# Scores by blocks of 32 keys, earlier stores of y, and x's tiles given up in pairs, in a hybrid decoder layer

## The chip, the cores and the metric

The kernel runs on one core of one Trainium2 chip. The metric is the device time of one execution in microseconds. Every fence marked as profile shows lines of a hardware profile of one execution.

## What is computed

One decoder layer (depth 1) for 512 prompt tokens and 8 x 8 sample tokens, 576 tokens (T) together, model width 2048, everything in float32:

```
xn   = RMSNorm(x)
proj = xn @ w_in                        # q, k, v, g, low-rank gate, z, x/B/C, dt
GLA (4 heads, key 128, value 256):
  b   = cumsum(log-gate) inside a chunk
  att[t,s] = sum_k q[t,k] * exp(b[t,k]-b[s,k]) * k[s,k]     for s <= t only
  o   = q*exp(b) @ S + att @ v,  S carried from chunk to chunk
SSD (16 heads of 64, state 128): the same kind of chunked scan, then norm
mix  = [o ; y] @ w_out ;  h = x + RMSNorm(mix)
out  = h + RMSNorm((silu(conv(h_n @ ffn_in))_a * (...)_b) @ ffn_out)
```

The kernel works with chunks of 128 tokens. The change concerns the matrix `att` of each chunk and head, the storing of y (the output of the SSD part) and its loading back for `@ w_out`.

## The kernel before, in words

**Main stream.** TensorE runs one long stream of projection products: for a tile of 128 output channels, 16 k-tiles of x (8 per "unit"), each with three products in fp32r (w_hi x_hi, w_hi x_lo, w_lo x_hi; lines 944 and 946) over two halves of 288 tokens. So a unit is 48 matmuls. Weights come by DMA from SyncE (line 361), ScalarE makes `w_hi` (line 441), GpSimd makes `w_lo` (line 383), in a ring of four slots. `units_done` counts finished units.

**Gaps.** The 32 tiles z, q, k, g, v (loop over `n < BESIDE`) have 63 "gaps", one after each unit, in which the small work of SSD and GLA is put into TensorE's stream. Every engine has its own `gap(m)` function with its part of gap m; `before_gap` puts small pieces between the k-tiles. Order on each engine is program order. ScalarE's queue also issues DMAs. An issue of a DMA waits in program order, but does not wait until the activations ahead of it have run.

**Scores.** In gaps 37, 39, ..., 51 `att_step(s)` (line 1109), s from 0 to 7, makes for each of 4 heads and 4 chunks one plain float32 matmul of 128 keys by 128 queries (line 1121). Step 0 is the diagonal. Step s multiplies operands scaled to a reference at block size m = LEVELS[s-1] = 64, 32, 16, 8, 4, 2, 1: only queries in the upper half of a block of 2m with keys in the lower half are wanted. VectorE takes those by a predicated copy with mask s (`take_att`, line 1670) and leaves the rest of PSUM unread. A float32 matmul of the program appears as two MATMUL records and two LDWEIGHTS records.  Four of the steps have a small part for the sample tokens too (line 1128).

**y.** `y_high(g)` (ScalarE, line 567) makes the high parts of four tiles of y; low parts come from GpSimd (line 402) for g = 0 and VectorE (line 1814) for g = 1. In gap 32 ScalarE does `y_high(0)`, `gates()` (the gate logits out of PSUM, lines 560 and 561, TensorE's part at line 1104), `y_high(1)`. In gap 33 come exp and ln of the gate. In gap 34 `y_low_out(0)`, `y_low_out(1)` store the low parts (line 571, 1152 KB each). In gap 35 `load_over_y(0)`, `load_over_y(1)` load q and k from `spill` over the place of the low parts (line 584; each waits until its own low part has landed in `y_spill`), and then `y_high_out(0)`, `y_high_out(1)` store the high parts (line 575). `att_step(0)` waits for q and k (`qk_in`, 32).

**y back.** The output projection reads y from the first eight k-tiles of `x_hi`/`x_lo`. SyncE waits at line 368 until the last unit that reads x's tiles 0 to 7 is done (`units_done`, OUT_UNIT0 - 1; it is the first half of tile n = 31), and then issues eight loads of 576 KB, in four pairs of k-tiles (lines 371 and 373), ahead of the next weights. TensorE's first `half_tile` of the output projection waits for pair k/2 before k = 0, 2, 4, 6. Between these two stands the second unit of tile 31, which reads x's tiles 8 to 15.

Of the kernel before, what the change touches and what calls it, by code (L numbers as in the profile page):

```python
# [52 lines left out]
CH = 128  # L53
# [56 lines left out]
def build(nc, xT, weights, vecs, ident_d, masks_d, gate2, sconv_in, fconv_in, fvec_d, gla_in,  # L110
# [4 lines left out]
    with ExitStack() as ctx:  # L115
# [151 lines left out]
        sq_ready, sq_used = sem("sq_ready"), sem("sq_used")  # L267
        root_ready = sem("root_ready")
        rstd_ready = sem("rstd_ready")
        gate_mm, gate_out, gate_exp, gate_ln = (sem(n) for n in ("gate_mm", "gate_out", "gate_exp", "gate_ln"))  # L270
        b_ready = sem("b_ready")
        v_tr, v_out = sem("v_tr"), sem("v_out")
        spilled = [sem("spilled0"), sem("spilled1")]
# [72 lines left out]
        @block.sync  # L346
        def _(sp):

            sp.dma_start(xin[0], xT[0]).then_inc(x_in[0], 16)
            sp.dma_start(raw[:, 0], weights[0]).then_inc(raw_in[0], 16)  # L350
            sp.dma_start(xin[1], xT[1]).then_inc(x_in[1], 16)
            sp.dma_start(raw[:, 1], weights[1]).then_inc(raw_in[1], 16)
            for c in (2, 3):
                sp.dma_start(xin[c], xT[c]).then_inc(x_in[2], 16)

            def weights_in(start, stop):

                with sp.Fori(start, stop) as i:
                    for j in range(2):
                        sp.wait_ge(lo_ready, 2 * i + j - 1)  # L360
                        sp.dma_start(raw[:, j], weights[bass.ds(2 * i + j, 1)].rearrange("o p a b -> (o p) a b"))\
                            .then_inc(raw_in[j], 16)

            weights_in(1, (OUT_UNIT0 + 4) // 2)
            sp.wait_ge(y_kept, 32)
            for g in range(SG):
                sp.wait_ge(ylo_kept[g], 16)
            sp.wait_ge(units_done, OUT_UNIT0 - 1)
            for i in range(4):
                a, z = 2 * i, 2 * i + 2  # L370
                sp.dma_start(x_hi[:, a:z, :].bitcast(F32), y_spill[0, a:z].rearrange("n p t -> p n t"))\
                    .then_inc(yb_in[i], 16)
                sp.dma_start(x_lo[:, a:z, :].bitcast(F32), y_spill[1, a:z].rearrange("n p t -> p n t"))\
                    .then_inc(yb_in[i], 16)
            weights_in((OUT_UNIT0 + 4) // 2, UNITS // 2)
# [59 lines left out]
        def _(act):  # L435
# [136 lines left out]
                    .then_inc(ylo_kept[g], 16)  # L572

            def y_high_out(g):
                act.dma_start(y_spill[0, 4 * g:4 * g + 4].rearrange("n p t -> p n t"), yh[:, 4 * g:4 * g + 4, :])\
                    .then_inc(y_kept, 16)

# [38 lines left out]
            def gap(m):  # L616
# [37 lines left out]
                if m == GAP_GATE:  # L654
                    for j in range(2):
                        act.wait_ge(hs_out[j], 16 * BATCHES // 2)
                    y_high(0)
                    gates()
                    y_high(1)
                if m == GAP_GATE + 1:  # L660
                    act.wait_ge(gate_out, GH)
                    nc.scalar.activation(GE2, GE2, ACT.Exp, scale=-1.0).then_inc(gate_exp, 1)
                    act.wait_ge(gate_exp, 1)
                    nc.scalar.activation(GE2, GE2, ACT.Ln, bias=1.0).then_inc(gate_ln, 1)
                if m == GAP_GATE + 2:
                    for g in range(SG):
                        y_low_out(g)
                if m == GAP_GATE + 3:
                    for g in range(SG):
                        load_over_y(g)  # L670
                    for g in range(SG):
                        y_high_out(g)
                if GAP_ATT <= m < GAP_ATT + 14 and (m - GAP_ATT) % 2 == 0:
                    level((m - GAP_ATT) // 2 + 1)
                if m == GAP_ATT + 14:
# [261 lines left out]
        def _(pe):  # L937
# [9 lines left out]
                                          start=False, stop=last)  # L947
                return mm

            def project(tile, unit, slot, ring, split=HALF, before=None, middle=None, behind=2, between=None):  # L950

                pe.wait_ge(taken, tile - behind + 3)
                for half in range(2):
# [3 lines left out]
                    for k in range(8):  # L957
                        kt = 8 * half + k
                        if before:
                            before(kt)  # L960
                        mm = products(slot + half, k, ring, split, kt == 0, kt == KT - 1, x_hi[:, kt], x_lo[:, kt])
                        if k == 7:
                            mm.then_inc(units_done, 1)
                        if between:
                            between(half, k)

# [129 lines left out]
            def gate(h):  # L1096
# [9 lines left out]
                                          misc[32:32 + RANK, n * HALF:(n + 1) * HALF], start=True, stop=True)  # L1106
                mm.then_inc(gate_mm, 1)

            def att_step(s):

                k, q = (GKK, GQ) if s == 0 else (GE, GE) if s % 2 else (GE2, GE2)
# [6 lines left out]
                for h in range(GH):  # L1118
                    for c in range(NC):
                        at = h * T + c * CH  # L1120
                        mm = nc.tensor.matmul(work[:, h, c * CH:(c + 1) * CH], k[:, at:at + CH], q[:, at:at + CH],  # L1121
                                              start=True, stop=True)
                    mm.then_inc(att_mm, 1)
                if s in SAMPLE_STEPS:
                    pe.wait_ge(att_out, att_base(s) + 1)
# [157 lines left out]
            for n in range(BESIDE):  # L1283
                tile = N_TILE0 + n
                project(tile, 2 * tile, 2 * tile % 4, tile % 2, middle=(lambda: gap(2 * n - 1)) if n else None,
                        between=lambda half, k: before_gap(2 * n - 1 + half, k))
                gap(2 * n)


# [149 lines left out]
        def _(ve):  # L1439
# [205 lines left out]

            def gates():

                ve.wait_ge(gate_ln, 1)
                own(tt_op(GE, GB, GE2, ALU.subtract))
                settle()  # L1650

# [538 lines left out]
```

## Time and profile before

| | us |
|---|---|
| median of 3 runs | 2717.47 (2716.44 to 2717.69) |
| the profiled execution, time | 2718.59 |
| its span | 2716.4 |
| TensorE matmul, busy | 2670.3 (98%) |
| VectorE, ScalarE, GpSimd busy | 45%, 28%, 39% |

Busy times are those of records; matmuls are pipelined, so a record (0.29 us) is longer than the distance to the next start (0.13 us). Below, the distance between starts is what a matmul costs. Idle time is time with no record open on an engine, and the profile names what it takes to have ended it.

### The profile page before, as it was taken

How to read it: one execution, taken by the hardware profiler on the slowest of the kernel's cores; microseconds unless marked ns; L12 is line 12 of the kernel's file. 1: busy time of each engine (PE TensorE's matmuls, PEld its weight loads, DVE VectorE, ACT ScalarE, POOL GpSimd, SP SyncE). 2: the span in 40 equal slices, each digit the busy share in tenths (PEclk: the TensorE clock that was granted, in tenths of full speed). 3: DMA queues.
4: the chain of work that ended last, by engine and by line, in shares of the span. 5: the costliest groups of instructions: out<-in, count | busy, mean ns of one | idle time of the engine just before them, and what ended most of it. 6: DMA issues, size and time to landing. Idle time of an engine off the chain costs nothing.

```text
span 2716.4 us, 48489 instructions
## 1 busy us (share of the span) xinstructions
PE 2670.3 (98%) x20130; PEld 2644.1 (97%) x20130; DVE 1218.1 (45%) x1459; ACT 763.0 (28%) x1225; POOL 1052.4 (39%) x458
## 2 busy tenths in 40 slices
PE   8999999999999999999999999999999999999996
PEld 7999999999999999999999999999999999999996
DVE  6644544654236354444333443444333443444436
ACT  6232222423214234222222222222222222222222
POOL 3332222423223354344433343444433443434347
PEclk9999999999999999999999999999999999999998
DMA  5222246422453423232222222222222222232224
GB/s 177 78 92 88 80 156 212 177 63 72 138 207 95 148 82 126 78 94 85 80 78 86 78 85 87 78 94 86 81 77 84 78 89 83 78 94 86 86 78 167
DMA packets 84645, 277.04 MB, mean 102 GB/s; under 512 B 9072, under 2 KB 13808, under 8 KB 83584
## 3 DMA queue, kind: packets, MB, share of 16 engines
q1 hardware_dynamic: 58336, 211.84, 24.8%
q10 hardware_dynamic: 26144, 62.64, 6.3%
q8 instruction: 148, 2.42, 0.4%
q14 instruction: 17, 0.14, 0.0%
HBM read 242.80 MB, written 31.65 MB: 101 GB/s over the span
## 4 chain that ended last, share of the span: by engine, by line
issue 44%; PE 31%; POOL 19%; DVE 2%; DMA 2%; ACT 1%; POOLq 0%; SPq 0%; ACTq 0%; DVEq 0%
POOL w_lo L383 18%; PE psum_proj L944 17%; PE psum_proj L946 8%; PE psum_work L1121 1%; POOL arena L414 1%; POOL arena L431 1%; DMA x_lo<-y_spill 1%; DVE arena L1875 1%; PE psum_work L1092 1%; POOL arena L422 1%; PE psum_work L1082 0%; DMA arena<-spill 0%; PE psum_work L1192 0%; DMA out_ssd_s_dram<-arena 0%; PE psum_work L1047 0%
## 5 line engine op out<-in xcount | busy, mean ns | idle before, releaser
L383 POOL TENSOR_TENSOR w_lo<-raw,w_hi 128x1024 fp32r<-128x1024 f32 x386 | 978.2, 2545 | 1642.4 <-ACT w_hi L441 1636.4
L944 PE MATMUL psum_proj<-x_hi,w_hi 128*128 128x288 f32 (+2 forms) x3104 | 934.8, 301 | 19.4 <-DVE x_lo L1464 13.0
L944 PE MATMUL psum_proj<-x_lo,w_hi 128*128 128x288 f32 (+2 forms) x3104 | 916.3, 295 | 0.0
L946 PE MATMUL psum_proj<-x_hi,w_lo 128*128 128x288 f32 (+2 forms) x3104 | 915.8, 295 | 0.0
L441 ACT ACTIVATE w_hi<-raw 128x1024 fp32r<-128x1024 f32 x386 | 398.0, 1053 | 892.4 <-PE psum_proj L946 494.9
L944 PEld LDWEIGHTS psum_proj<-x_hi,w_hi 128*128 128x128 f32 x3104 | 588.3, 190 | 27.6 <-issue 15.5
L944 PEld LDWEIGHTS psum_proj<-x_lo,w_hi 128*128 128x128 f32 x3104 | 584.9, 188 | 3.4 <-issue 1.9
L946 PEld LDWEIGHTS psum_proj<-x_hi,w_lo 128*128 128x128 f32 x3104 | 584.5, 188 | 0.0
L944 PE MATMUL psum_work<-x_lo,w_hi 128*128 128x256 f32 (+1 forms) x1408 | 414.7, 294 | 0.0
L944 PE MATMUL psum_work<-x_hi,w_hi 128*128 128x256 f32 (+1 forms) x1408 | 414.5, 294 | 0.0
L946 PE MATMUL psum_work<-x_hi,w_lo 128*128 128x256 f32 (+1 forms) x1408 | 414.4, 294 | 0.0
L840 ACT ACTIVATE arena<-arena 128x592 f32<-128x592 f32 x88 | 77.8, 884 | 747.3 <-DVE arena L1949 747.3
L944 PEld LDWEIGHTS psum_work<-x_hi,w_hi 128*128 128x128 f32 x1408 | 267.0, 190 | 0.0
L946 PEld LDWEIGHTS psum_work<-x_hi,w_lo 128*128 128x128 f32 x1408 | 264.3, 188 | 0.0
L944 PEld LDWEIGHTS psum_work<-x_lo,w_hi 128*128 128x128 f32 x1408 | 264.2, 188 | 0.0
L1947 DVE TENSOR_TENSOR arena<-psum_proj,rstd 128x512 f32<-128x512 f32 x44 | 30.4, 691 | 428.7 <-PE psum_proj L946 428.7
L944 PE MATMUL psum_proj<-g_lo,w_hi 128*128 128x288 f32 x672 | 198.3, 295 | 0.0
L944 PE MATMUL psum_work<-g_lo,w_hi 128*128 128x288 f32 x672 | 198.2, 295 | 0.0
L946 PE MATMUL psum_proj<-g_hi,w_lo 128*128 128x288 f32 x672 | 198.1, 295 | 0.0
L946 PE MATMUL psum_work<-g_hi,w_lo 128*128 128x288 f32 x672 | 198.1, 295 | 0.0
L944 PE MATMUL psum_work<-g_hi,w_hi 128*128 128x288 f32 x672 | 197.3, 294 | 0.1
L944 PE MATMUL psum_proj<-g_hi,w_hi 128*128 128x288 f32 x672 | 197.1, 293 | 0.0
(311 smaller groups left out, 3249.4 us busy)
## 6 DMA issues: line engine op xcount, KB each, us to landing
raw<-in_weights_dram SPq DMA_DIRECT2D x386, 512.0 KB, 3.6
spill<-tail ACTq DMA_DIRECT2D x24, 288.0 KB, 2.1
arena<-in_xT_dram SPq DMA_DIRECT2D x4, 1152.0 KB, 10.6
y_spill<-arena ACTq DMA_DIRECT2D x4, 1152.0 KB, 10.8
h_spill<-arena ACTq DMA_DIRECT2D x4, 1152.0 KB, 4.5
x_hi<-h_spill ACTq DMA_DIRECT2D x1, 4608.0 KB, 17.8
out_yT_dram<-arena ACTq DMA_DIRECT2D x8, 576.0 KB, 3.5
arena<-in_ssdT_in_dram ACTq DMA_DIRECT2D x8, 512.0 KB, 5.9
```

Source lines behind the costliest of these rows:

```text
L383: nc.gpsimd.tensor_tensor(w_lo[:, slot], raw[:, r], w_hi[:, slot].bitcast(F32), ALU.subtract).then_inc(lo_ready, 1)
L414: nc.gpsimd.tensor_tensor(mixT[:, kt], mixT[:, kt], xres(kt), ALU.add).then_inc(h_w, 1)
L422: nc.gpsimd.tensor_tensor(cut(fsum, n), cut(fsq[0] if kt == 1 else fsum, n), cut(fsq[kt % 2], n), ALU.add).then_inc(ysq_sum, 1)
L431: nc.gpsimd.tensor_tensor(a, a, cut(x_hi[:, kt].bitcast(F32), n), ALU.add).then_inc(y_wp, 1)
L441: nc.scalar.activation(w_hi[:, slot], raw[:, r], ACT.Copy).then_inc(hi_ready, 1)
L840: nc.scalar.activation(ftap[j % 2][:, 0:FCONVW], pd[:, 0:FCONVW], ACT.Identity, bias=fc[q][:, 4 * j + 3:4 * j + 4], scale=fc[q][:, 4 * j:4 ...
L944: nc.tensor.matmul(banks[:, n, 0:b - a], w_hi[:, slot, k], (hi, lo)[part][:, a:b], start=first and part == 0, stop=False)
L946: mm = nc.tensor.matmul(banks[:, n, 0:b - a], w_lo[:, slot, k], hi[:, a:b], start=False, stop=last)
L1092: mm = nc.tensor.matmul(work[:, j // 4, j % 4 * SN:(j % 4 + 1) * SN], xw[0:SMP, j * P:(j + 1) * P], Bm[:, b, j // 4, :], start=True, stop= ...
L1121: mm = nc.tensor.matmul(work[:, h, c * CH:(c + 1) * CH], k[:, at:at + CH], q[:, at:at + CH], start=True, stop=True)
L1875: nc.vector.reciprocal(r, r).then_inc(grs, 1)
L1947: tt_op(pd[:, FC - 1:FC - 1 + SEQ].rearrange("p (n t) -> p n t", n=2), banks[:, :, 0:256], rstd[:, 0:SEQ].rearrange("p (n t) -> p n t", n= ...
```

## The change

Three parts, in the diff in this order of lines.

(a) Stores of y. `y_high_out(0)` follows `y_high(0)` at once, `y_low_out(0)` follows the gates, `y_high_out(1)` follows `y_high(1)`, `y_low_out(1)` comes behind exp and ln in gap 33, `load_over_y(0)` is in gap 34, `load_over_y(1)` in gap 35. A wait for `yhi` is put before each store of a high part, and one semaphore is reused for exp and ln.

(b) Scores. `att_step` makes, in place of one matmul of 128 keys by 128 queries, 2 or 4 matmuls of up to 32 keys: for m = 64 two of 32 keys by 64 queries; for m = 32 two of 32 by 32; for smaller m four of (32 - m) by (32 - m); for step 0 four of 32 by 32. All contract over 128 rows.

(c) x's tiles. In the first unit of tile 31 `x_read` is raised behind k = 1, 3 and 5, and SyncE waits for it before pairs 0, 1 and 2; pair 3 waits for `units_done` as before.

```diff
-            sp.wait_ge(units_done, OUT_UNIT0 - 1)
             for i in range(4):
                 a, z = 2 * i, 2 * i + 2
+                sp.wait_ge(*((x_read, i + 1) if i < 3 else (units_done, OUT_UNIT0 - 1)))
                 sp.dma_start(x_hi[:, a:z, :].bitcast(F32), y_spill[0, a:z].rearrange("n p t -> p n t"))\
                     .then_inc(yb_in[i], 16)
...
             def y_high_out(g):
+                act.wait_ge(yhi, 4 * g + 4)
                 act.dma_start(y_spill[0, 4 * g:4 * g + 4].rearrange("n p t -> p n t"), yh[:, 4 * g:4 * g + 4, :])\
                     .then_inc(y_kept, 16)
...
                     y_high(0)
+                    y_high_out(0)
                     gates()
+                    y_low_out(0)
                     y_high(1)
+                    y_high_out(1)
                 if m == GAP_GATE + 1:
                     act.wait_ge(gate_out, GH)
-                    nc.scalar.activation(GE2, GE2, ACT.Exp, scale=-1.0).then_inc(gate_exp, 1)
-                    act.wait_ge(gate_exp, 1)
+                    nc.scalar.activation(GE2, GE2, ACT.Exp, scale=-1.0).then_inc(gate_ln, 1)
+                    act.wait_ge(gate_ln, 1)
                     nc.scalar.activation(GE2, GE2, ACT.Ln, bias=1.0).then_inc(gate_ln, 1)
+                    y_low_out(1)
                 if m == GAP_GATE + 2:
-                    for g in range(SG):
-                        y_low_out(g)
+                    load_over_y(0)
                 if m == GAP_GATE + 3:
-                    for g in range(SG):
-                        load_over_y(g)
-                    for g in range(SG):
-                        y_high_out(g)
+                    load_over_y(1)
...
+                        if given_up and half == 0 and k in (1, 3, 5):
+                            mm.then_inc(x_read, 1)
...
+            def kept_blocks(s):
+
+                m = LEVELS[s - 1] if s else 0
+                if m == 64:
+                    return [(a, a + 32, 64, CH) for a in (0, 32)]
+                if m == 32:
+                    return [(a, a + 32, a + 32, a + 64) for a in (0, 64)]
+                return [(a, a + 32 - m, a + m, a + 32) for a in (0, 32, 64, 96)]
...
                         at = h * T + c * CH
-                        mm = nc.tensor.matmul(work[:, h, c * CH:(c + 1) * CH], k[:, at:at + CH], q[:, at:at + CH],
-                                              start=True, stop=True)
+                        for a, z, a_q, z_q in kept_blocks(s):
+                            mm = nc.tensor.matmul(work[a:z, h, c * CH + a_q:c * CH + z_q], k[:, at + a:at + z],
+                                                  q[:, at + a_q:at + z_q], start=True, stop=True)
                     mm.then_inc(att_mm, 1)
...
-                ve.wait_ge(gate_ln, 1)
+                ve.wait_ge(gate_ln, 2)
```

## Rows read from the trace of the kernel before

**Rows 1.** The page's first part: each engine's busy us, share of the span, instructions.
```profile
PE 2670.3 (98%) x20130; PEld 2644.1 (97%) x20130; DVE 1218.1 (45%) x1459; ACT 763.0 (28%) x1225; POOL 1052.4 (39%) x458
```

**Rows 2.** Whom TensorE waited for, one line: us in total, times, longest us.
```profile
PE psum_proj L944 <- DMA x_lo<-y_spill: 4.4, 2, 3.5
```

**Rows 3.** TensorE's timeline around score step 1: start us, us, engine, line, operation, count.
```profile
542.05 3.73 PE L1121 MATMUL psum_work<-arena 128*128 128x128 f32 x32
545.54 0.38 PE L944 MATMUL psum_proj<-x_hi,w_hi 128*128 128x288 f32 x1
```

**Rows 4.** TensorE's timeline, matmuls with 64 columns of weights on alternating halves of PSUM's rows.
```profile
247.64 1.09 PE L1043 MATMUL psum_work<-arena 128*64 128x128 f32 x16
248.66 1.12 PE L1047 MATMUL psum_work<-tail,arena 128*128 128x512 f32 x2
...
385.32 0.30 PE L944 MATMUL psum_proj<-x_lo,w_hi 128*128 128x288 f32 x1
385.45 0.29 PE L946 MATMUL psum_proj<-x_hi,w_lo 128*128 128x288 f32 x1
385.68 1.15 PE L1069 MATMUL psum_work<-arena 64*64 64x64 f32 x32
386.76 0.40 PE L944 MATMUL psum_proj<-x_hi,w_hi 128*128 128x288 f32 x1
```

**Rows 5.** TensorE's timeline, short transposes (16 rows, 16 columns moving), two of ten.
```profile
200.45 0.21 PE L1234 MATMUL psum_work<-ident,tail 16*128 16x16 f32 x1
200.51 0.21 PE L1234 MATMUL psum_work<-ident,misc 16*128 16x16 f32 x1
```

**Rows 6.** ScalarE's queue and engine, gaps 34 and 35.
```profile
504.56 1.19 ACTq L571 DMA_DIRECT2D y_spill<-arena  x2
...
511.90 4.41 ACTq L584 DMA_DIRECT2D arena<-spill  x2
```

**Rows 7.** Line 571's own view: time from issue to landing of its two stores.
```profile
DMA to landing us min/median/max: 7.3/9.1/10.8
```

**Rows 8.** The issues view: KB each, median us to landing.
```profile
arena<-spill ACTq DMA_DIRECT2D x2, 1152.0 KB, 8.3
```

**Rows 9.** TensorE's timeline, score step 0 with the idle time before it.
```profile
524.36 3.81 PE L1121 MATMUL psum_work<-arena 128*128 128x128 f32 x32 [2.01 <-POOL w_lo L383]
```

**Rows 10.** Two windows: busy of PE, PEld, DVE, ACT, POOL, then granted clock, DMA share, GB/s.
```profile
500.00:504.00 4.00, 4.00 (x33) 4.00 (x32) 2.10 (x4) 3.97 (x3) 3.02 (x1) 1.00 0.00 0
...
508.00:512.00 4.00, 4.00 (x32) 4.00 (x31) 3.96 (x2) 1.53 (x2) 3.46 (x1) 1.00 1.05 413
```

**Rows 11.** Timeline of gap 32: ScalarE's high parts and first gate copies, TensorE's third gate matmul.
```profile
487.86 2.41 ACT L567 ACTIVATE arena<-arena 128x576 fp32r<-128x576 f32 x4 [1.53 <-DVE tail L1856]
...
490.80 0.73 ACT L561 ACTIVATE tail<-psum_work,vec 128x576 f32<-128x576 f32 x1
...
491.80 1.23 PE L1104 MATMUL psum_work<-misc,tail 16*128 16x288 f32 x4
```

**Rows 12.** SyncE's queue: the last weights before y (two issues), and the first load of y.
```profile
721.94 15.93 SPq L361 DMA_DIRECT2D raw<-in_weights_dram  x2
742.45 0.40 SPq L371 DMA_DIRECT2D x_hi<-y_spill  x1
```

**Rows 13.** TensorE's timeline where the output projection begins, rows with idle time.
```profile
756.11 0.40 PE L944 MATMUL psum_proj<-x_hi,w_hi 128*128 128x288 f32 x1 [0.91 <-DMA x_lo<-y_spill]
...
762.20 0.40 PE L944 MATMUL psum_proj<-x_hi,w_hi 128*128 128x288 f32 x1 [3.46 <-DMA x_lo<-y_spill]
```

**Rows 14.** Windows, columns as in rows 10, at the output projection and at the mix norm.
```profile
755.00:762.20 7.20, 2.84 (x22) 2.65 (x21) 0.00 (x0) 0.00 (x0) 0.00 (x0) 1.00 1.04 413
...
762.84:769.76 6.92, 6.92 (x33) 6.92 (x31) 3.75 (x6) 1.06 (x1) 2.38 (x1) 0.51 0.25 67
...
988.00:992.00 4.00, 4.00 (x21) 3.59 (x19) 0.34 (x4) 0.20 (x2) 0.39 (x1) 0.57 0.43 131
```

**Rows 15.** TensorE's timeline before the second of those: one-column matmuls.
```profile
986.03 1.45 PE L1335 MATMUL psum_work<-ones,tail 128*128 128x1 f32 x12 [0.71 <-DVE tail L1902]
```

More of the change, by code:

```diff
@@ L269, in build @@
         rstd_ready = sem("rstd_ready")
-        gate_mm, gate_out, gate_exp, gate_ln = (sem(n) for n in ("gate_mm", "gate_out", "gate_exp", "gate_ln"))
+        gate_mm, gate_out, gate_ln, x_read = (sem(n) for n in ("gate_mm", "gate_out", "gate_ln", "x_read"))
         b_ready = sem("b_ready")
@@ L948, in products, with project @@
                 return mm
-            def project(tile, unit, slot, ring, split=HALF, before=None, middle=None, behind=2, between=None):
+            def project(tile, unit, slot, ring, split=HALF, before=None, middle=None, behind=2, between=None,
+                        given_up=False):
                 pe.wait_ge(taken, tile - behind + 3)
@@ L1285, in _ @@
                 project(tile, 2 * tile, 2 * tile % 4, tile % 2, middle=(lambda: gap(2 * n - 1)) if n else None,
-                        between=lambda half, k: before_gap(2 * n - 1 + half, k))
+                        between=lambda half, k: before_gap(2 * n - 1 + half, k), given_up=n == BESIDE - 1)
                 gap(2 * n)
```

## The prediction

> **What bounds the kernel now.** First the page's shares: TensorE's matmuls are open for 98% of the span, every other engine is under half [rows 1]. So time can come only from TensorE's own instructions, from its few idle stretches, and from its clock. Then the view of whom TensorE waited for, cut to the two waits near the change: 4.4 us for the loads of y [rows 2] and 2.0 us ahead of a score step [rows 9]. Then the timeline and the windows there, for what these waits are made of.
>
> The 2.0 us stand before score step 0 [rows 9]. The profile names GpSimd's `w_lo`, but I read them as a wait for k. ScalarE's two low stores go out at 504.56 and about 505.1, and the second takes 10.8 us to land [rows 6, 7], so 515.9. The two loads of q and k are 4.41 us apart though one issue takes 0.4 us [rows 6]: the second is held until its low part has landed, and goes out near 515.9. With 8.3 us to land [rows 8] it is there at 524.2, and TensorE starts at 524.36 [rows 9]. The DMA engines are full at this time (share 1.05, 413 GB/s) [rows 10].
>
> The 4.4 us are two waits of the first half tile of the output projection, 0.91 and 3.46 us [rows 13]. SyncE issued the first load at 742.45, and the last data are there at 762.2; the end of that stretch is DMA at 413 GB/s [rows 12 to 14]. A cost follows that no list of waits shows: behind the 3.46 us of idleness the granted clock is 0.51 for 6.92 us [rows 14], the lower of the two levels (1.2 GHz for 2.4).
>
> **Part (b), the scores.** Before: a step of 16 float32 matmuls, 32 records, takes 545.54 - 542.05 = 3.49 us, 109 ns each [rows 3]; eight steps are 27.9 us, all in TensorE's stream and so all on the path. After: steps 0 and 3 to 7 have 16 x 4 matmuls, 128 records, steps 1 and 2 have 16 x 2, 64 records; 896 records in place of 256. Less work, many more instructions: with 0.1 us for the entry of each step (below), 896 t + 0.8 us = 27.9 us holds at t = 30 ns. All hangs on t.
>
> No row shows a float32 matmul with 32 columns of weights. The nearest have 64 and alternate between two halves of PSUM's rows: with 64 columns moving 32 records take 386.76 - 385.68 = 1.08 us, 34 ns each; with 128 moving 16 take 248.66 - 247.64 = 1.02 us, 64 ns each [rows 4]. That is 0.47 ns for a moving column and 4 ns fixed, or 19 ns at 32 columns and 12 ns at 16; over the widths here (16 to 32) some 17 ns. So 34 ns is the upper end, 17 ns the lower. The lower one supposes that no price per instruction shows up first; the upper is measured, with twice the columns. I take 25 ns, the middle. For step 1 (64 columns moving) I take the row's 34 ns. Entering a narrow group costs more: 385.68 - 385.45 = 0.23 us where two starts are else 0.13 us apart [rows 4]; so 0.1 us for each step. Leaving shows in both kernels.
>
> At 25 ns: six steps of 128 x 25 ns + 0.1 = 3.30 us, less by 0.19 each, -1.1; step 1 is 64 x 34 ns + 0.1 = 2.28, -1.2; step 2 is 64 x 25 ns + 0.1 = 1.70, -1.8. Sum **-4.1 us**. At 17 ns it is -10.8, at 34 ns for all +3.4. VectorE still takes a head after TensorE's signal for it and is 45% busy, so nothing there becomes late.
>
> The Trainium skill ("TensorE: Matmul & The Clock Gate", the section on why a gap is 56 and not 53.3 ns) says that starts never come closer than about 25 ns, and, where firmware decodes, that the sequencer spends about 62 ns on each matmul. By the first, part (b) would be near the -4.1 us. By the second a step of 128 would be 7.9 us and the kernel would be slower by some 19 us. The 34 ns of rows 4 speak against the second, but only over 32 matmuls, which may have stood decoded ahead; this is the first rival below, priced there from a row.
>
> **Part (a), the stores.** Nothing is added to the DMA traffic; 4.6 MB move earlier. The first high store goes out when the high parts are made, at 487.86 + 2.41 = 490.3, the first low one behind the gates near 496, the second high one near 500, the second low one near 505 as before, since it now stands behind exp. There is free DMA time before: 500 to 504 shows none used at all in the window view, and the engines fill only from 508 on [rows 10]. The low store of part 1 now shares them with the q load alone, and I let it land in 6 us (between 10.8 and the low end of 7.3 less a share of the traffic [rows 7]): 511. The k load goes out then and takes at most the 8.3 us of now [rows 8]: 519.3. TensorE asks for it at 524.36 - 2.01 = 522.35. So the **2.0 us go**, with 3 us to spare; if only 1 us of the 4.9 came, all would stay. What is late next there is nothing that I find: weights (next in ScalarE's queue) arrive sooner in the emptier DMA.
>
> What it costs: ScalarE's sequencer now waits for `yhi` and issues a DMA (about 0.55 us, half of the 1.09 to 1.19 us for two [rows 6]) between the high parts and the gate copies. Queued behind are all of `gates()`. The first head's copies end at 490.80 + 0.73 = 491.53 today, and TensorE's third gate matmul, which waits for them, starts at 491.80 [rows 11]: 0.27 us of slack. Copies 0.75 us later make TensorE wait **0.5 us** (0 to 0.8). The other added issues stand before `w_hi`, which is units ahead of TensorE; they cost nothing while that lead lasts, up to 0.6 us each if not. Part (a): **-1.5 us** (-2.0 to +0.5).
>
> **Part (c), x's tiles.** SyncE's last weight issue before y ends at 721.94 + 15.93 = 737.87 [rows 12], then it waits 4.6 us. Pair 0, 1 and 2 are given up 6, 4 and 2 k-tiles before the end of the unit, each at least 6 x 0.13 = 0.8 us: before 737.4, 739.0 and 740.6. So pairs 0 to 2 go out between 737.9 and 741.6 and only pair 3 at 742.45. Data to move until then: eight loads of 576 KB, 4.7 MB, and 1 to 1.5 MB of weights and states. At 413 GB/s [rows 14] 4.7 + 1.5 = 6.2 MB are 15 us from 737.9, so the last lands by 753, 9 us before now. TensorE needs pair 0 at 756.11 - 0.91 = 755.2, and pair 3 at 762.20 - 3.46 - 0.91 = 757.8. Both waits go, **-4.4 us**, with 2 us and more to spare. With them goes the idleness and so the slow stretch: 6.92 x (1 - 0.51) = 3.4 us at most, of which I take **3.2**, since fixed parts of a matmul do not scale. SyncE issues the next weights behind y's loads as before, earlier if anything. Part (c): **-7.6 us** (-4.0 if a rest of 1 to 2 us of waiting and the slow stretch stay).
>
> **Sum.** -4.1 - 1.5 - 7.6 = -13.2 us on the profiled execution's 2718.59 us (its span is 2716.4, with 2.2 us around it), 2705.4. The median of the runs is 1.1 us lower, 2717.47, so I predict **2704.3 us**.
>
> **Rivals.** *The instruction rate decides* (slower). A score step now is 128 matmuls and as many weight loads in a row; rows 4 show a fast stretch of only 32. If the sequencer feeds a long row of them more slowly than TensorE eats, t is its rate. For: transposes of 16 columns, with next to nothing to stream, start 0.06 us apart [rows 5]. Against: those load 128 columns of weights, which explains them as well. At 60 ns six steps cost 4.3 us more each, the two others 0.4: +26.7, in all +17.6, **2735 us**. It decides from t = 40 ns on, where the gains of (a) and (c) are used up; over 0.2% slower from 46 ns.
>
> *The clock falls in the score steps* (slower). After 0.7 us of idleness and 1.45 us of one-column matmuls the clock was 0.57 over the next four microseconds [rows 14, 15], so thin matmuls do not hold it. If 3.3 us of 32-column matmuls on a quarter of the array act alike, each of six steps is followed by a slow stretch like that of rows 14, 3.2 us: +19.2, **2723.5 us**. Against: here columns stream all the time.
>
> *The waits are only moved* (little changes). y's loads or k land late all the same, since weights and states share a full DMA, or the scores cost the full 34 ns: -4.1 + 0 - 1 or +3.4 - 1.5 - 7.6: **2712 us**.
>
> **How the numbers follow.** Forecast 0.70, instruction rate 0.12, clock 0.07, waits moved 0.11. The forecast's own ends: -10.8 - 2.0 - 7.8 = -20.6, 2697; and +3.4 + 0.5 - 4.0, 2717. The range 2695 to 2716 holds it and most of the third rival, and leaves the two slow ones out. A measurement of this kernel can tell about 0.2% (5.4 us) from no change. Faster: the forecast almost whole and half of the third rival, 0.74; same 0.10; slower 0.16.
>
> **What would show it.** Right: score steps with 128 records take 2.3 to 4.4 us and those with 64 under 2.3; no idle row before score step 0; no idle row at the first half tile, and a clock of 1.00 from 755 to 770; about 0.5 us of idleness at the third gate matmul. Wrong: steps of 6 us or more (rate), a clock under 1.00 in the 7 us behind a step (clock), an idle row with y's loads still there (waits moved).

## The result, and the profile after

The changed kernel takes 2695.26 us in the median of its runs (2692.86 to 2696.11), the kernel before on the same chip 2717.58. The ratio is 0.9911, with a 95% interval of 0.9899 to 0.9922: 22.3 us by the medians, 24.2 us by the ratio (21.2 to 27.4), where 13.2 were forecast. The profiled execution took 2695.66 us. Line numbers of the changed kernel are higher by 1 to 14 than those of before.

The page, its first lines and TensorE's row (before in rows 1). TensorE has 640 matmul records more and is open 18.8 us less:

```profile
span 2693.5 us, 49769 instructions
...
PE 2651.5 (98%) x20770; PEld 2624.1 (97%) x20770; DVE 1220.2 (45%) x1459; ACT 763.2 (28%) x1225; POOL 1055.8 (39%) x458
```

To see where the time went, the same instruction is looked up in both traces. Its start in the one less its start in the other is the gain up to there:

| first start of | before | after | difference | of this stretch |
|---|---|---|---|---|
| third gate matmul (gap 32) | 491.80 | 493.06 | +1.3 | +0.9 was there before the change's first edit, +0.3 is a new wait |
| score step 0 | 524.36 | 523.55 | -0.8 | -2.1, part (a): the idle 2.0 us before the step are gone |
| transposes of k (gap 53) | 663.61 | 647.30 | -16.3 | -15.5, part (b): -17.1 for the steps, +0.4 and +1.2 for waits on VectorE |
| first GLA chunk (gap 56) | 684.9 | 670.2 | -14.7 | +1.6, a slow clock |
| first matmul of `keep_clock` (mix norm; its results are not used) | 982.5 | 959.8 | -22.7 | -8.0, part (c) |
| end of the span | 2716.4 | 2693.5 | -22.9 | -0.2 |

The score steps, TensorE's timeline (start us, us, engine, line, operation, count), each with the start of what follows it; before in rows 3. The distance is what a step costs: 1.35, 1.91, 1.14, 1.21 and 1.35 us here (steps 0, 1, 2, 3 and 7), with 128, 64, 64, 128 and 128 records. So records start 10.5, 29.8, 17.8, 9.5 and 10.5 ns apart. Before, it was 3.49 us in the four steps without a sample part and 3.66 to 3.74 in the four with one:

```profile
523.55 1.35 PE L1135 MATMUL psum_work<-arena 128*32 128x32 f32 x128
525.33 0.68 PE L1142 MATMUL psum_work<-arena 128*64 128x64 f32 x8 [0.43 <-DVE arena L1684]
...
539.38 1.98 PE L1135 MATMUL psum_work<-arena 128*32 128x64 f32 x64
541.29 0.40 PE L945 MATMUL psum_proj<-x_hi,w_hi 128*128 128x288 f32 x1
...
554.73 1.21 PE L1135 MATMUL psum_work<-tail 128*32 128x32 f32 x64
555.87 0.40 PE L945 MATMUL psum_proj<-x_hi,w_hi 128*128 128x288 f32 x1
...
569.30 1.28 PE L1135 MATMUL psum_work<-arena 128*16 128x16 f32 x128
570.51 0.40 PE L945 MATMUL psum_proj<-x_hi,w_hi 128*128 128x288 f32 x1
...
629.40 1.34 PE L1135 MATMUL psum_work<-arena 128*31 128x31 f32 x128
630.75 0.68 PE L1142 MATMUL psum_work<-arena 128*64 128x64 f32 x8
```

(Step 0 ends at 525.33 - 0.43 = 524.90.) All eight steps are 10.9 us in place of 28.7, 17.8 less. Each now starts 0.22 to 0.23 us behind the projection matmul ahead of it, where that was 0.13, which takes 0.7 back: 17.1 us.

Whom TensorE waited for (us in total, times, longest). The two waits for y [rows 2] are gone from the list. New are a wait before the sample part of step 0, for VectorE's copy of the first head, and one at the gates, and the wait before the transposes of k has grown from 1.3 to 2.4 us:

```profile
PE psum_work L1164 <- ACT arena L687: 2.4, 1, 2.4
...
PE psum_work L1142 <- DVE arena L1684: 0.4, 1, 0.4
PE psum_work L1108 <- ACT tail L561: 0.3, 1, 0.3
```

Windows around that grown wait and around the start of the output projection (busy of PE, PEld, DVE, ACT, POOL, granted clock, DMA share, GB/s; before in rows 14). Behind the wait the clock is 0.57 for 4 us, which is lost time that did not exist there before. At the output projection it is now 1.00 and TensorE has no idle time:

```profile
645.00:648.00 3.00, 0.69 (x7) 0.73 (x8) 0.96 (x3) 1.59 (x3) 0.08 (x1) 1.00 0.52 124
648.00:652.00 4.00, 4.00 (x22) 4.00 (x21) 0.00 (x0) 2.41 (x5) 2.36 (x1) 0.57 0.34 123
...
740.00:745.00 5.00, 5.00 (x42) 5.00 (x42) 0.27 (x2) 0.00 (x0) 0.00 (x0) 1.00 1.03 417
745.00:750.00 5.00, 5.00 (x42) 5.00 (x41) 3.84 (x6) 1.07 (x1) 2.40 (x1) 1.00 0.41 99
```

ScalarE's queue in the same gaps as rows 6:

```profile
491.20 0.38 ACTq L576 DMA_DIRECT2D y_spill<-arena  x1
...
497.28 0.38 ACTq L571 DMA_DIRECT2D y_spill<-arena  x1
...
500.97 0.37 ACTq L576 DMA_DIRECT2D y_spill<-arena  x1
...
505.99 0.37 ACTq L571 DMA_DIRECT2D y_spill<-arena  x1
...
507.02 1.31 ACTq L585 DMA_DIRECT2D arena<-spill  x1
...
512.53 0.37 ACTq L585 DMA_DIRECT2D arena<-spill  x1
```

The view of line 585, its last line:

```profile
DMA to landing us min/median/max: 8.8/9.4/10.1
```

The second load, k, goes out at 512.53 instead of near 515.9 and is there by 522.6 at the latest. TensorE starts step 0 at 523.55 without a wait.

SyncE's queue, loads of y. The first pair goes out at 723.54; the fourth, which still waits for the end of the unit, at 727.69. Before, all eight loads waited for that end [rows 12], so against it the first pair now goes out some 4.2 us earlier (727.69 - 723.54). The last load is issued at 728.10, and by the view of line 373 (at most 13.7 us from issue to landing) it is there by 741.8; TensorE comes to the last pair at 742.63:

```profile
723.54 0.39 SPq L371 DMA_DIRECT2D x_hi<-y_spill  x1
...
727.69 0.36 SPq L371 DMA_DIRECT2D x_hi<-y_spill  x1
```

What ends the grown wait is a chain on VectorE. Its timeline behind step 7: masked copies, differences for k's decay, k times decay, q times decay, the copy of decays, the next projection tile; then ScalarE's copy of v and TensorE's transposes:

```profile
629.94 2.62 DVE L1684 COPY_PREDICATED arena<-masks,psum_work 128x512 f32<-128x512 uint8 x4 [4.25 <-PE psum_work L1135]
...
632.77 2.82 DVE L1713 TENSOR_TENSOR arena<-arena 128x2048 f32<-128x2048 f32 x2
637.79 2.56 DVE L1716 TENSOR_TENSOR arena<-arena 128x2304 f32<-128x2304 f32 x1 [2.20 <-ACT arena L678]
640.26 2.55 DVE L1719 TENSOR_TENSOR arena<-arena,tail 128x2304 f32<-128x2304 f32 x1
642.73 2.38 DVE L1720 COPY decay<-tail 128x16 f32<-128x16 f32 x1
...
645.24 0.76 DVE L1870 TENSOR_TENSOR tail<-psum_proj,rstd 128x576 f32<-128x576 f32 x1
...
647.30 2.98 PE L1164 MATMUL psum_work<-ident,arena 128*128 128x128 f32 x16 [2.43 <-ACT arena L687]
```

Before, VectorE took a head of scores as TensorE finished it, 0.9 us apart, and was done 4.8 us after the step began. Now its four copies in a row take 2.6 us and it is done after 3.5 us. TensorE gains 2.1 us in the step and 2.3 by the end of the unit behind it, VectorE 1.4 us with its copies and 1.1 by the time it takes the next projection tile (15.8 us after the step's start, before 17.0). The difference, 1.2 us, comes out as waiting.

### The profile page after: what moved, and what is told of

It reads as the page before. It is cut to its first block, busy times and chain, and to the rows that moved or that the text cites. A ratio compares the mean times of both kernels' runs of the same rounds, so it can differ in the third digit from the quotient of the medians.

```text
span 2693.5 us, 49769 instructions
## 1 busy us (share of the span) xinstructions
PE 2651.5 (98%) x20770; PEld 2624.1 (97%) x20770; DVE 1220.2 (45%) x1459; ACT 763.2 (28%) x1225; POOL 1055.8 (39%) x458
## 4 chain that ended last, share of the span: by engine, by line
issue 44%; PE 31%; POOL 19%; DVE 3%; DMA 1%; ACT 1%; POOLq 0%; ACTq 0%; SPq 0%; DVEq 0%
PE psum_proj L945 17%; POOL w_lo L383 17%; PE psum_proj L947 8%; POOL arena L414 1%; POOL arena L431 1%; DVE arena L1889 1%; PE psum_work L1096 1%; POOL arena L422 1%; PE psum_work L1206 0%; DMA arena<-spill 0%; PE psum_work L1086 0%; DMA out_ssd_s_dram<-arena 0%; PE psum_work L1135 0%; PE psum_work L1051 0%; PE psum_work L1029 0%
```

## The experiments

The theory from the two traces: the three parts work in three separate stretches. In part (b) each group of 32 columns of the array streams by itself, and groups run side by side; a block's group is the rows of PSUM that it is written to (0, 32, 64 or 96 up). What is left to gain is in VectorE's chain behind step 7.

### One part at a time

**only_scores**: the kernel before with part (b) alone (`kept_blocks` as in the change).

```diff
-                        mm = nc.tensor.matmul(work[:, h, c * CH:(c + 1) * CH], k[:, at:at + CH], q[:, at:at + CH],
-                                              start=True, stop=True)
+                        for a, z, a_q, z_q in kept_blocks(s):
+                            mm = nc.tensor.matmul(work[a:z, h, c * CH + a_q:c * CH + z_q], k[:, at + a:at + z],
+                                                  q[:, at + a_q:at + z_q], start=True, stop=True)
```

> The kernel before with part (b) alone (scores by blocks). Theory: the three parts act in three separate stretches and add up; the records of a score step start 9 to 10 ns apart with four groups of columns, 18 ns with two groups and 32 queries, 30 ns with two groups and 64 queries, whatever the stores do. Then this kernel is 14 us faster than the one before (12 to 16), the idle 2.0 us before step 0 and the two waits for y of 4.4 us stay, and the wait before the transposes of the keys grows from 1.3 to about 2.4 us. Rival: some of the gain seen between step 0 and those transposes came from the emptier DMA of part (a); then this kernel is under 12 us faster.

Measured: 2702.16 us against 2718.88 before, ratio 0.9938 (0.9921 to 0.9954), so 16.7 us by the medians, a little over the 12 to 16 expected. The rival falls. The waits for y are there (4.4 us), and the wait before k's transposes is 2.4 us as foreseen.

**only_stores**: the kernel before with part (a) alone. The first lines of its edit, the rest as in the change:

```diff
                     y_high(0)
+                    y_high_out(0)
                     gates()
+                    y_low_out(0)
                     y_high(1)
+                    y_high_out(1)
```

> The kernel before with part (a) alone (stores of y as made). Theory: k's load is what ends the idle time before score step 0, so it goes (2.0 us) and 0.3 us come at the third gate matmul: 1.7 us faster (0.5 to 2.5), with k landed less than 2 us before TensorE asks for it. Rival: the idle time was for w_lo, as the profile names it; then 1 us or more of it stays, since those weights land late here too.

Measured: 2714.79 us against 2718.88, ratio 0.9984 (0.9975 to 0.9994). By the starts of instructions in the trace, part (a) gives 1.8 us between the second gate matmul and step 0 in that execution, and no idle time is left before step 0, although GpSimd begins the `w_lo` there at 522.48 and step 0 starts at 522.84: the theory holds, the rival falls. The 4.1 us of the medians are more than the 0.5 to 2.5 expected (the ratio's interval is 1.6 to 6.8 us). In the traced execution another 1.4 us came from the clock at a place that part (a) does not touch: the idle 3.55 us before y were followed by a granted clock of 0.75 over 6.92 us, where the execution of before had 0.55 over as long a stretch. The next experiment shows another reason.

**only_tiles**: the kernel before with part (c) alone (one semaphore is reused for exp and ln, as in the change, to free one for `x_read`, which is raised as in the change).

```diff
-            sp.wait_ge(units_done, OUT_UNIT0 - 1)
             for i in range(4):
                 a, z = 2 * i, 2 * i + 2
+                sp.wait_ge(*((x_read, i + 1) if i < 3 else (units_done, OUT_UNIT0 - 1)))
```

> The kernel before with part (c) alone (x's tiles given up in pairs). Theory: both waits for y (0.9 and 3.5 us) go and with them the stretch of 6.9 us at a granted clock of 0.51: 7.5 to 8.2 us faster, clock 1.00 from 755 to 770. Rival: the clock falls for another reason than the idle time; then 4.4 us faster and the clock is under 1.00 still.

Measured: 2713.19 us against 2718.88, ratio 0.9977 (0.9967 to 0.9986), 5.7 us, less than the 7.5 to 8.2 expected. Both waits for y are gone, and the granted clock from 755 to 770 is 1.00. Between the first GLA chunk and the mix norm this execution gained 8.0 us on the one before (from 3.5 behind to 4.5 ahead), as the theory says. It had lost the 3.5 us earlier, at a place that part (c) does not touch. TensorE's timeline there:

```profile
526.41 5.30 PE L1124 MATMUL psum_work<-arena 128*128 128x128 f32 x32 [2.91 <-issue]
```

Two windows around it, columns as above:

```profile
520.00:526.00 6.00, 3.50 (x27) 3.27 (x25) 3.52 (x4) 2.21 (x3) 2.41 (x2) 1.00 1.02 381
526.00:530.00 4.00, 3.59 (x19) 3.62 (x20) 0.77 (x2) 1.19 (x1) 2.31 (x1) 0.57 1.04 416
```

ScalarE's queue with its two loads, grouped in one row:

```profile
513.01 4.38 ACTq L584 DMA_DIRECT2D arena<-spill  x2
```

The view of their line, its last line:

```profile
DMA to landing us min/median/max: 8.5/8.9/9.3
```

The second load goes out near 517.0 and takes at most 9.3 us: 526.3, and TensorE starts at 526.41. Here the profile does not name `w_lo` any more, which was done by then (at 524.55). It was done in the trace of before too, at 523.42, 0.9 us ahead of the start that the profile puts down to it:

```profile
521.05 2.37 POOL L383 TENSOR_TENSOR w_lo<-raw,w_hi 128x1024 fp32r<-128x1024 f32 x1 [5.20 <-ACT w_hi L441]
```

So k's load is what ends this wait, as the prediction read it. And the wait is 2.9 us here, with the clock at 0.57 behind it, where the execution of before had 2.0 us and a clock of 1.00. only_scores shows the same: 2.49 us and 0.62 from 526 to 530. So part (a) takes away 2.0 to 2.9 us of waiting and, in some executions, some 1.5 us of slow clock too. That fits its 4 us in the medians better than the one trace does; how often the clock falls there was not counted.

The three ratios apart add up to 27.5 us (2718.88 x (0.0062 + 0.0016 + 0.0023)), and the ratio of the whole change gives 24.2. The intervals of the three are about 4.5, 2.7 and 2.6 us to either side, so the 3 us between the two lie within them: the parts do not help each other, and whether they take anything from each other can't be told.

### What makes the scores cheap

Three kernels take apart what the blocks changed at once: narrow weight loads, fewer queries, and four groups of columns.

**one_group**: the same matmuls, all written to the same rows of PSUM, so that one group of columns does them all. The blocks overwrite each other, so part of the scores is left out. The next three kernels have one execution each, so what they show is read from the starts in their traces.

```diff
-                            mm = nc.tensor.matmul(work[a:z, h, c * CH + a_q:c * CH + z_q], k[:, at + a:at + z],
+                            mm = nc.tensor.matmul(work[0:z - a, h, c * CH + a_q:c * CH + z_q], k[:, at + a:at + z],
```

> The changed kernel with all score blocks written to the first rows of PSUM (partitions 0 up), so that all use one group of columns of the array; the scores are wrong by this, the number, the shapes and the operands of the matmuls are unchanged. Theory (each group streams by itself, at 2 cycles a column plus some 8 ns, and groups run side by side): records start 30 to 40 ns apart in every step of 32 columns, a step of 128 records takes 4 to 5 us in place of 1.25, the kernel gets some 20 us slower than the changed one. Rival (small matmuls are cheap by themselves, the price is per record and column): still 9 to 12 ns apart.

Measured: 2709.26 us, 14 us slower than the changed kernel where some 20 were expected. TensorE's timeline, steps 1 and 3:

```profile
541.36 3.76 PE L1135 MATMUL psum_work<-arena 128*32 128x64 f32 x64
545.05 0.40 PE L945 MATMUL psum_proj<-x_hi,w_hi 128*128 128x288 f32 x1
...
574.06 3.37 PE L1135 MATMUL psum_work<-arena 128*16 128x16 f32 x128
577.36 0.40 PE L945 MATMUL psum_proj<-x_hi,w_hi 128*128 128x288 f32 x1
```

A record costs 3.69 us / 64 = 57.6 ns with 64 columns moving and 3.30 / 128 = 25.8 ns with 16; step 0 (32 columns) took 4.16 us, 32.5 ns. So the theory holds for 28 to 64 columns, with a fixed part of 4 to 6 ns and not 8; with 24 columns (3.31 us, 25.9 ns) and 16 the price stays near 26 ns, and a step of 16 columns missed the 4 to 5 us expected. The eight steps take 28.4 us, 17.5 more than in the changed kernel; 1.2 us of the wait before k's transposes, the 0.4 us in step 0 and the 1.6 us of slow clock are gone in exchange, which leaves 14.3.

**groups_in_turn**: the blocks in the outer loop, so one group does 8 records before the next group's turn.

```diff
-                    for c in range(NC):
-                        at = h * T + c * CH
-                        for a, z, a_q, z_q in kept_blocks(s):
+                    for a, z, a_q, z_q in kept_blocks(s):
+                        for c in range(NC):
+                            at = h * T + c * CH
```

> The changed kernel with the loops of the score blocks exchanged: the same group of columns for all four chunks (8 records), then the next group. Theory 1 (matmuls start strictly in order, so only neighbours of different groups overlap): records 25 to 35 ns apart, a step of 128 records 3 to 4.5 us. Theory 2 (the engine starts a group's matmul past a waiting one of another group): 9 to 12 ns apart as in the changed kernel, 1.2 to 1.5 us.

Measured: 2697.19 us. Step 3:

```profile
570.86 2.17 PE L1135 MATMUL psum_work<-arena 128*16 128x16 f32 x128
572.95 0.40 PE L945 MATMUL psum_proj<-x_hi,w_hi 128*128 128x288 f32 x1
```

2.09 us for 128 records, 16.3 ns; step 0 took 2.64 us, 20.6 ns. Neither theory gave this: eight records of one group in a row are 8 x 32.5 = 260 ns on that group, and they pass in 165. So the next group's records start before the eight of the last group are through, but the four groups do not all run at once; how far the overlap reaches is left open. Going round the groups is right: 10.5 ns against 20.6. The whole kernel shows little of it (18.3 us for the eight steps in place of 10.9, but only 1.9 us more in the time of its one execution), in part because the wait before k's transposes shrinks from 2.4 to 1.3 us, with no slow clock behind it.

**all_queries**: 32 keys by all 128 queries in four groups, in every step.

```diff
-                        for a, z, a_q, z_q in kept_blocks(s):
+                        for a in (0, 32, 64, 96):
```

> The changed kernel with blocks of 32 keys by all 128 queries, four groups, 128 records in every step: the work of the kernel before, cut by keys only. Theory (2 cycles a column per group, four groups side by side): 107 ns and some 10 to 20 more for a record in its group, 29 to 32 ns apart, a step 3.7 to 4.2 us, a little over the 3.49 of the kernel before; so the gain of part (b) comes from the columns left out and the groups together. Rival (the gain comes from the narrow weight loads alone): 1.3 to 2 us as in the changed kernel.

Measured: 2708.78 us. Step 1:

```profile
540.92 3.70 PE L1135 MATMUL psum_work<-arena 128*32 128x128 f32 x128
544.55 0.40 PE L945 MATMUL psum_proj<-x_hi,w_hi 128*128 128x288 f32 x1
```

3.63 us, 28.4 ns a record, 113 ns within its group. So the rival (narrow loads alone) falls, and the theory's low end was 0.1 us high. The four cases together, for the eight steps: whole 128 x 128 matmuls 28.7 us; blocks in one group 28.4; four groups with all queries 29.0; both 10.9. Neither half of the idea gains anything alone over the eight steps. A single step can: step 2, with only two blocks, took 2.14 us in one group.

### VectorE's chain behind step 7

**late_queries**: in the changed kernel, q's decay and the copies of the decays come one gap later, behind the next projection tile.

```diff
                 tt_op(GE, GE, GKK, ALU.mult).then_inc(kdT_ready, 1)
+
+            def decay_of_queries():
+
                 ve.wait_ge(exp_ready, 9)
...
+                if m == GAP_ATT + 15:
+                    decay_of_queries()
```

> The changed kernel with one thing moved: VectorE's scaling of q by its decay and the two copies of the decays (5 us of work behind score step 7) come after it has taken the next projection tile, one gap later. Theory: the changed kernel's new limit behind step 7 is VectorE's chain (masked copies, decays, q, two copies, tile, then ScalarE's copy of v, then TensorE's transposes of k): the wait of 2.4 us goes, and with it the stretch at a granted clock of 0.57 behind it; 3.5 to 4.5 us faster than the changed kernel, that is 26 to 28 us faster than the kernel before. Rival: ScalarE or GpSimd is as late as VectorE there; then the wait shrinks by under 1 us, and the time by as much.

Measured: 2690.3 us against 2718.88, ratio 0.9895 (0.9879 to 0.9912), 28.6 us by the medians, a little over the 26 to 28 expected. VectorE's timeline: the projection tile comes at 640.14, where the changed kernel had it at 645.24. TensorE's list of waits has no wait before k's transposes any more:

```profile
640.14 0.75 DVE L1875 TENSOR_TENSOR tail<-psum_proj,rstd 128x576 f32<-128x576 f32 x1
640.81 4.70 DVE L1722 TENSOR_TENSOR arena<-arena,tail 128x2304 f32<-128x2304 f32 x1
```

**changed_again** and **late_queries_again** set the two side by side on one chip.

> The changed kernel again, on the same chip as late_queries again and the kernel before, to set the three side by side. Theory (the parts add up, less what VectorE's chain behind step 7 takes back): 22 to 25 us faster than before, idle 2.4 us ahead of the transposes of k again, with the clock fallen behind it. Rival (the idle time there was one execution's): under 1.5 us idle and 26 us faster or more.

> late_queries again, on the same chip as the changed kernel. Theory: 4 to 6 us faster than the changed kernel, the interval clear of it. Rival: the difference seen was the chip's; then under 2 us.

Measured: 2694.52 us (2692.74 to 2696.82, ratio 0.9912, 0.9898 to 0.9925) and 2690.65 us (2689.56 to 2692.60, ratio 0.9894, 0.9878 to 0.9909), before 2718.48. The difference is 3.9 us, a little under the 4 to 6 expected. The intervals of the two ratios overlap. The executions do not: the highest of all eight of late_queries is 2692.60, the lowest of all nine of the changed kernel 2692.74. By the starts in the traces, score step 0 to k's transposes is 121.2 us in both executions of late_queries and 123.8 in both of the changed kernel, so 2.6 us belong to the move. The wait of 2.4 us was there again, but this time with the clock at 1.00 behind it:

```profile
648.00:652.00 4.00, 4.00 (x34) 4.00 (x33) 0.00 (x0) 1.56 (x4) 2.04 (x1) 1.00 0.40 102
```

So the wait belongs to the change, and the slow clock behind it, worth 1.6 us, comes in some executions only. The two executions shown here differ by only 0.1 us in time, mostly since the one of late_queries took 2.6 us longer behind the mix norm, which the move does not touch.

### The same cut elsewhere

**split_reads**: late_queries, with the reads of the carried states for the sample tokens cut into four groups, in the SSD part and in the GLA part, 32 pieces each. The edit of the GLA part, the other is alike:

```diff
-                    mm = nc.tensor.matmul(work[:, 0, n * SMP + b * DEC:n * SMP + (b + 1) * DEC],
-                                          s0_slots[b][:, h, vh * P:(vh + 1) * P], GQ[:, at:at + DEC],
+                    for r in range(0, P, 32):
+                        mm = nc.tensor.matmul(work[r:r + 32, 0, n * SMP + b * DEC:n * SMP + (b + 1) * DEC],
+                                              s0_slots[b][:, h, vh * P + r:vh * P + r + 32], GQ[:, at:at + DEC],
```

> late_queries, and the reads of the carried states for the sample tokens (64 pieces of 4 records, weights 128 columns, 8 columns moving) cut into four groups of 32 columns, 16 records each. Theory (records of few columns in four groups start 9.5 ns apart, entering and leaving a narrow stretch costs 0.1 us each): a piece costs 0.35 us in place of 0.45, 6 us faster in all, 34 us faster than the kernel before. Rival (changing the width of the array's columns costs more for short pieces): 0.45 us or more for a piece, no gain or a loss.

Measured: 2693.32 us against 2720.41, ratio 0.9905 (0.9889 to 0.9922), where 34 us were expected: no gain on late_queries. One piece in TensorE's timeline:

```profile
735.60 0.29 PE L947 MATMUL psum_proj<-x_hi,w_lo 128*128 128x288 f32 x1
735.82 0.31 PE L1208 MATMUL psum_work<-arena 128*32 128x8 f32 x16
736.06 0.40 PE L945 MATMUL psum_proj<-x_hi,w_hi 128*128 128x288 f32 x1
736.30 0.29 PE L945 MATMUL psum_proj<-x_lo,w_hi 128*128 128x288 f32 x1
...
739.75 0.40 PE L945 MATMUL psum_proj<-x_hi,w_hi 128*128 128x288 f32 x1 [1.15 <-DMA x_lo<-y_spill]
```

From 735.60 to 736.30 are 0.70 us, of which two plain distances are 0.26: 0.44 us for the piece, as with 4 wide records (0.71 and 0.45 in the changed kernel). 0.2 of it is entering and leaving, and 16 records in 0.24 us are 15 ns each, not 9.5. The rival holds: so short a piece does not pay. The last row shows something else: a wait for y is back, 1.15 us. The last load of y was issued at 724.48 and took at most 15.2 us (the view of line 373), so it landed by 739.7, and TensorE came to it at 738.60, 14.1 us after the issue. The changed kernel has 14.5 us there and its loads take at most 13.7. Part (c) has 0.8 us to spare, and why the load took longer here was not tried.

## Why the prediction was wrong

Of the sum -4.1 - 1.5 - 7.6, two terms held and one was a quarter of what it should have been. The measured ratio puts the time just past the low end of the range: 0.9911 of the 2717.47 us of before is 2693.3, and the range began at 2695 (the median of the changed kernel, 2695.26, is at that edge). The forecast's own fast end was 2697.

**Part (b), the price t of a record: the step that failed.** The prediction took 25 ns, between 17 and 34. Measured are 9.5 to 10.5 ns in the six steps with four groups, 17.8 ns in step 2, 29.8 ns in step 1. The extrapolation itself was good where it applied: its line (0.47 ns a column and 4 ns) gives 19 ns at 32 columns for two alternating groups, and step 2, which has two groups, has 17.8. What I did not do is ask what the two rows were bounded by. Both were two groups side by side, so their prices were already halves: one_group shows 57.6 ns for 64 columns where the changed kernel's step 1 has 29.8. The trace of before could have told it. The sample part of a score step has 8 records with the same 64 columns of weights and 64 moving as rows 4, but all on the same half of PSUM's rows (and contracting over 128 rows, not 64), and takes 76 ns for each in place of 34 (some 64 without the 0.1 us for leaving):

```profile
630.60 0.68 PE L1128 MATMUL psum_work<-tail 128*64 128x64 f32 x8
631.21 0.40 PE L944 MATMUL psum_proj<-x_hi,w_hi 128*128 128x288 f32 x1
```

With four groups the half becomes a quarter, 32.5 / 4 = 8 ns, and a floor of some 10 ns shows first (what sets it was not tried). "17 ns is the lower end" was thus no lower end, and taking the middle of the range moved the term further off. With 10 ns in the six steps and the rest of the sum as it stands, part (b) would have been -15.7. Measured are -17.1 before VectorE's share and -15.5 after it; of the rest, 0.8 us is that the 27.9 us took all eight steps for the 3.49 of one, and 0.7 that steps 1 and 2 also cost less than priced.

**"Nothing there becomes late" on VectorE** also failed, by its size. 45% busy over the span says nothing of the chain behind one step. It took 1.2 us back as idle time behind step 7, 0.4 in step 0, and up to 1.6 us as slow clock. Moving 5 us of VectorE's work out of that chain returned 3.9 us by the medians, since the 1.3 us that TensorE had waited there before went too.

**Part (a)**: forecast -1.5, measured -2.1 at step 0 and +0.3 at the gates in the trace, and more in the medians. The reading of k's load against the `w_lo` that the profile names held, shown by only_tiles and only_scores. The 0.5 us at the third gate matmul came as 0.29. The landing was less comfortable than I put it: the load took up to 10.1 us, not 8.3, and 1 us was spare, not 3. The DMA engines were still full from 510 to 520 (share 1.00 to 1.06).

**Part (c)**: forecast -7.6, measured -8.0 in the change and in only_tiles and -7.1 in changed_again (where 0.7 us more of other waiting stands in that stretch), with both the waits and the slow clock gone. Its slack was overrated: 0.8 us at the last pair, not 2 and more, and split_reads waits 1.15 us again. One reading was off without harm: the wait that ends at 756.11 is for the third pair (it stands behind the fourth k-tile of the half tile), so pair 0 is needed some 3.5 us before the 755.2 that the prediction gives it.

**The rivals.** The instruction rate does not decide: 128 records, with as many weight loads, come 10 ns apart over 1.3 us. The page "TensorE: Matmul & The Clock Gate" of the Trainium skill (the section on why a gap is 56 and not 53.3 ns) says that starts are never closer than about 25 ns, and that each matmul costs about 62 ns where firmware decodes. The rows of this case show 9.5 ns between records in different groups of columns, and 25.8 ns within one group, so the figure of 25 fits one group and not four. The same page of the Trainium skill, in its part on packing small matmuls, has tiles start some 4 ns apart. The 9.5 ns are nearer to that. The clock did not fall in the score steps or behind them: every window of 4 us from 522 to 638 has a granted clock of 1.00. What the prediction read from rows 14 and 15 for this rival, that thin matmuls do not hold the clock, does not stand either: behind the same 0.71 us of idleness and the same 1.45 us of one-column matmuls, the next four microseconds have 0.60 in the execution of before (987.40 to 991.40) and 1.00 in that of changed_again (963.40 to 967.40). The waits were not moved to y or k, but a new one came where I had not looked.

## What to carry to other kernels

When a matmul of many columns is cut to what a mask keeps, put neighbouring pieces in different groups of 32 columns and go round the groups: a record then costs its group's time divided by the groups, down to some 10 ns in this kernel, and neither the cut nor the groups gained anything alone over the eight steps here. Before a price is taken from a row, ask how many units worked side by side in that row. And when TensorE's part of a chain shrinks, time the chain of the engine that answers it, from TensorE's signal to TensorE's next wait, instead of reading its busy share.

## What was unexpected of the hardware

One group of columns took 57.6 ns for a float32 record of 64 columns, 32.5 ns for 32, and 25.8 ns for 16; four groups in rotation 28.4 ns at 128 columns, 10.5 at 32 and 9.5 at 16. Entering a stretch of these narrow matmuls costs about 0.1 us (0.22 us between starts where 0.13 is usual), and so does leaving it. The leaving is no matter of narrowness: behind the whole 128 x 128 float32 matmuls of before it is 0.22 us too (545.54 to 545.76).

The slow clock is not a fixed consequence of an idle time. Idle 2.0 us left it at 1.00; 2.4 us were followed by 0.57 over four microseconds in one execution and by 1.00 in two others (changed_again, only_scores); 2.5 and 2.9 us by 0.62 and 0.57; 3.5 us by 0.55 over the next 6.92 us in one execution, by 0.50 in only_scores and by 0.75 in only_stores. At the mix norm 0.7 us and one-column matmuls were followed by 0.60 in one and 1.00 in another. What decides between the two was not found. The 0.50 is the lower of the two levels (1.2 GHz for 2.4) for the whole of the stretch, the others have it for part.

VectorE's copy of 128 x 16 decays took 2.38 us in the changed kernel and 0.16 in late_queries, where in its turn the product of q and its decay took 4.70 us instead of 2.55. The 2.2 us moved to the neighbour rather than went away. What beside the two holds VectorE up was not tried.
